# A two-block network in float32 on one core: the up units' activations turned by a VectorE block turn and ScalarE copies in place of TensorE transposes

## The chip, the cores and the metric

One core of a Trainium2 chip runs the whole kernel. The time is the device time of one launch in microseconds, the median of the runs. Five engines are named here: TensorE (PE, with its weight loads as PEld), VectorE (DVE), ScalarE (ACT), GpSimd (POOL) and SyncE (SP), which issues the weight DMAs.

## The reference, cut to what matters

Two blocks follow each other on 256 tokens of width 2048, in float32. The first is a gated mixture (linear attention and a short convolution) with a feed-forward part behind it; the second is an attention block with a layer norm. The change lies in the feed-forward part:

```python
h2 = rms_norm(x, g_ffn[l])
hid = jnp.square(jax.nn.relu(jnp.einsum('bsd,df->bsf', h2, w_ffn_up[l])))
x = x + jnp.einsum('bsf,fd->bsd', hid, w_ffn_down[l])
```

h2 is 256 x 2048, hid is 256 x 8192.

## The kernel before, in words

All large products have the same shape: 256 tokens by 2048 of contraction by 512 output columns. Such a product is a **unit**, and there are 96 of them, in the order of the list UNITS (lines 14 to 20). A unit has four **steps** of 512 of contraction, numbered s = 4u + c over the whole kernel. A step has 24 matmuls of 128x128 by 512: four tiles of contraction, two token halves, and three products, since each float32 operand is split into a high and a low part (hi x hi, hi x lo, lo x hi). The results of a unit stand in two PSUM banks, acc, one for each token half; two pairs of banks alternate.

The feed-forward part runs as four groups of four up units and four down units: up 0 to 3, down 0 to 3, up 4 to 7, down 0 to 3 again with the next 2048 of contraction, and so on.

For each step the four engines do this:

- SyncE loads 1 MB of weights, raw, three steps ahead; the load waits until VectorE has done the split of the buffer's last contents (L513).
- ScalarE makes whi, the rounded copy of raw (split, L674), two steps ahead. It waits for the load and until TensorE has left the buffer.
- VectorE makes wlo = raw - whi (split, L954).
- TensorE multiplies (products, L1390 to L1392).

Each engine goes through its own program in order. At stage s it first does split(s + 2), then what jobs(s) lists (from line 32), which is the same list for all engines. For a unit u that ends with step 4u + 3, the job "post" at that stage takes the result out of PSUM, and the table LATER (line 25) says which jobs follow at stages 4u + 4, 4u + 5 and so on. TensorE does its jobs behind the products of the same stage.

For an up unit, post is: ScalarE writes Relu of the first token half into a tmp buffer (L756) and VectorE that of the second (L1101), each scaled by the token's rstd; POOL squares the whole buffer in place (L625). The down units need the result with the features on the partitions, so the job turn_up at stage 4u + 4 turns it: TensorE makes eight 128x128 transposes into two of the four side banks (turn, L1400), ScalarE copies each bank as the high part into A_hi (hi_of, L679), VectorE subtracts to get the low part A_lo (lo_of, L961), and the bank is free again. The eight transposes stand between two steps of products in TensorE's order. The side banks are numbered in order of use by side_uses and SN.

The down units read A_hi and A_lo. The function ready gives the semaphore on which TensorE waits before it reads a part of a set for the first time: the first down unit of a group waits, at contraction tile kk, for the turn of up unit j + kk // 4, so for the group's fourth up unit at its own fourth step. The set is free for a group's up units when the last down unit of the group before is through (set_free). There are three tmp buffers, taken in turn; tmp_free gives the wait before one is written again.

Of the kernel before, what the change touches and what calls it, by code (L numbers as in the profile page):

```python
# [22 lines left out]


LATER = {"q": ("turn_qk",), "k": ("turn_qk",), "r": ("turn_r",), "cx": ("shift", "none", "conv0", "conv1"), "cb": ("turn_cb",),
         "yb": ("turn_yb",), "wo": ("turn_wo",), "up": ("turn_up",), "q2": ("none", "turn_qk2"),
         "k2": ("turn_qk2",), "y": ("none", "turn_y")}

LEVELS = (128, 64, 32, 16, 8, 4, 2, 1)
# [152 lines left out]
def two_block_program(nc, T, C, out):  # L182
# [8 lines left out]
    with ctx:  # L191
# [21 lines left out]
        whi = [at(f"whi{i}", "hi", 8 * KB * i, [128, 4, 512], f32r) for i in range(3)]  # L213
        wlo = [at(f"wlo{i}", "lo", 8 * KB * i, [128, 4, 512], f32r) for i in range(3)]

        A_hi, A_lo = (at("setA_" + n, "A", o, [128, 16, 256], f32r) for n, o in (("hi", 0), ("lo", 16 * KB)))
        B_hi, B_lo = (at("setB_" + n, "B", o, [128, 16, 256], f32r) for n, o in (("hi", 0), ("lo", 16 * KB)))

# [127 lines left out]
        s_rv, s_rq, s_ro, s_rx = sem("s_rv"), sem("s_rq"), sem("s_ro"), sem("s_rx")  # L346
        s_cw, s_shift, s_cu = sem("s_cw"), sem("s_shift"), sem("s_cu")
        s_yb, s_pq, s_xf = sem("s_yb"), sem("s_pq"), sem("s_xf")
        s_mb, s_nm, s_ex = sem("s_mb"), sem("s_nm"), sem("s_ex")
        s_pn, s_ph, s_pl = sem("s_pn"), sem("s_ph"), sem("s_pl")  # L350
        s_vh, s_yv, s_yh, s_yl = sem("s_vh"), sem("s_yv"), sem("s_yh"), sem("s_yl")
# [32 lines left out]
        def tmp_free(u):  # L384

            n = TN[u] - 3
            if n < 0:
                return s_lvl, 1
            kind, j = UNITS[TMPS[n]]
            if kind == "wo":  # L390
                return s_sq[1], 2 * j + 2
            if kind == "down":
                return s_sq[2], 2 * (j - 12) + 2
            if kind == "cc":
                return evacuated(TMPS[n] + 2)
            return full("turn", TMPS[n], 1)

        def hi_lo_of(u):
# [5 lines left out]
        def ready(u, kk):  # L404

            kind, j = UNITS[u]
            part = kk // 2
            if u == 0:
                return s_xl, kk + 1
            if kind == "ya" and j == 0:  # L410
                return seen("turn", UI["r", kk // 4], part % 2)
            if kind == "yb" and j == 0:
                return seen("turn", UI["cb", kk // 4], part % 2)
            if kind == "wo" and j == 0:
                return seen("turn", UI["yb", kk // 4], part % 2)
            if kind == "up" and j == 0:
                return seen("turn", UI["wo", kk // 4], part % 2)
            if kind == "down" and j % 4 == 0:
                return seen("turn", UI["up", j + kk // 4], part % 2)
            if kind == "q2" and j == 0:  # L420
                return seen("turn", UI["down", 12 + kk // 4], part % 2)
            if kind == "out" and j == 0:
                return s_yl, part + 1
            return None
# [43 lines left out]
        def asf(ap):  # L468
            return ap.bitcast(f32)
# [194 lines left out]
        def scalar(e):  # L664
# [37 lines left out]
            def copies(u, dst, scale):  # L702
                for b in range(2):
# [2 lines left out]
                    e.activation(dst[:, 2 * b:2 * b + 2, :], two(side[n % 4][:, :]), ACT.Copy,  # L706
                                 scale=scale).then_inc(s_read[n % 4], 1)

            def squares(u, i, j):
                tm = tmp_of(u)  # L710
                e.wait_ge(*evacuated(u))
                e.wait_ge(*tmp_free(u))
                for t in range(2):
                    e.activation(tm[:, t, :], X1[:, t, 512 * j:512 * j + 512], ACT.Square,
                                 accum_out=ssq[i][:, t, j:j + 1]).then_inc(s_sq[i], 1)
# [64 lines left out]
            for s in range(NS):  # L780
# [7 lines left out]
                for job, a in jobs(s):  # L788
# [80 lines left out]
                    elif job == "turn_cb":  # L869
                        j = UNITS[a][1]  # L870
                        e.wait_ge(*mm_done(UI["ya", 3]))
                        for b in range(2):
                            hi_of(("turn", a, b), B_hi[:, 4 * j:4 * j + 4, :], b)
                    elif job == "turn_y":
                        j = UNITS[a][1]
                        e.wait_ge(*set_free(a))
                        e.wait_ge(s_xf, 2)
                        e.wait_ge(*full("values", 11 if j < 2 else 15))
                        for b in range(2):
                            k = 4 * j + 2 * b  # L880
                            e.wait_ge(*seen("turn", a, b))
                            e.activation(A_hi[:, k:k + 2, :], YT[:, k:k + 2, :], ACT.Copy).then_inc(s_yh, 1)
                    elif job in ("turn_yb", "turn_up"):
                        j = UNITS[a][1] % 4
                        e.wait_ge(*set_free(a))
                        for b in range(2):
                            hi_of(("turn", a, b), A_hi[:, 4 * j:4 * j + 4, :], b)
                    elif job in ("turn_wo", "turn_x2"):
                        i, col = (1, G_FFN) if job == "turn_wo" else (2, G_FIN)
                        j = UNITS[a][1] % 4  # L890
                        squares(a, i, j)
                        e.wait_ge(*set_free(a))
                        for b in range(2):
                            hi_scaled(("turn", a, b), B_hi[:, 4 * j:4 * j + 4, :], col + 4 * j, b)
                        if j == 3:
                            root(i)
                    elif job == "turn_qk2":
                        kind, g = UNITS[a]
                        dst = (qTa if kind == "q2" else kTa)[g % 2]
                        if g >= 2:  # L900
                            e.wait_ge(*full("scores", 8 * (g - 2) + 7))
                        else:
                            e.wait_ge(s_xf, 2)
                        for b in range(2):
                            hi_of(("turn", a, b), dst[:, :, :], b)
                    elif job == "att":
                        if a % 2 and a >= 3 and not gate_turns(s):
                            one_half((a - 3) // 2)
                        for h in ((a - 2, a - 1) if a >= 2 and a % 2 == 0 else ()):
                            n = SN["probs", h]  # L910
                            e.wait_ge(*full("probs", h))
                            if h >= 2:
                                e.wait_ge(*full("values", h // 2 - 1))
                            e.activation(PT[h % 2][:, :, :], two(side[n % 4][:, :]), ACT.Copy).then_inc(s_ph, 1)
                        for h in ((a, a + 1) if a < 32 and a % 2 == 0 else ()):
                            b = h % 2
                            e.wait_ge(s_nm, h + 1)
                            for t in range(2):
                                e.activation(Sm[b][:, t, :], Sm[b][:, t, :], ACT.Exp, bias=nmx[b][:, t:t + 1],  # L919
                                             accum_out=den[b][:, t:t + 1]).then_inc(s_ex, 1)  # L920
                    elif job == "bank_ln":
                        e.wait_ge(s_ln, 32)
                        if a == 0:
                            for b in range(4):
                                last = max(n for n in SN.values() if n % 4 == b)
                                e.wait_ge(s_read[b], last // 4 + 1)
                        else:
                            e.wait_ge(*evacuated(UI["out", 2]))
                        for i in ((0, 1), (2,))[a]:
                            e.activation(gain_at[i], lngB[:, vcols[i]], ACT.Copy).then_inc(s_lb, 1)  # L930
                            e.activation(bias_at[i], lnbB[:, vcols[i]], ACT.Copy).then_inc(s_lb, 1)
                    elif job == "post":
                        post(a)
# [11 lines left out]
        def vector(e):  # L945
# [208 lines left out]
            def times_gate(u):  # L1154
                j = UNITS[u][1]
                e.wait_ge(*seen("values", 4 * j + 3))
                for b in range(2):
# [2 lines left out]
                    e.wait_ge(*full("turn", u, b))  # L1160
                    e.tensor_tensor(v, two(side[n % 4][:, :]), v, ALU.mult).then_inc(s_read[n % 4], 1)

            def finish(t):
                v, r, m = lvar[:, t:t + 1], lrs[:, t:t + 1], nmu[:, t:t + 1]
                e.wait_ge(s_dv, dv)
# [20 lines left out]
            for s in range(NS):  # L1186
# [17 lines left out]
                for job, a in jobs(s):  # L1204
# [101 lines left out]
                    elif job == "turn_y":  # L1306
# [3 lines left out]
                        for b in range(2):  # L1310
# [1 line left out]
                            e.wait_ge(s_yh, 2 * j + b + 1)  # L1312
                            e.tensor_tensor(A_lo[:, k:k + 2, :], YT[:, k:k + 2, :], asf(A_hi[:, k:k + 2, :]),
                                            ALU.subtract).then_inc(s_yl, 1)
                    elif job in ("turn_yb", "turn_up"):
                        j = UNITS[a][1] % 4
                        for b in range(2):
                            lo_of(("turn", a, b), A_lo[:, 4 * j:4 * j + 4, :], A_hi[:, 4 * j:4 * j + 4, :], b)
# [48 lines left out]
        def tensor(e):  # L1367
# [117 lines left out]
            for s in range(NS):  # L1485
# [6 lines left out]
                for job, a in jobs(s):  # L1492
# [37 lines left out]
                    elif job.startswith("turn"):  # L1530
# [2 lines left out]
                            e.wait_ge(s_rx, 2 * j + 2)  # L1533
                        elif kind == "yb":
                            e.wait_ge(s_yb, j + 1)
                        elif kind == "up":
                            e.wait_ge(s_pq, j + 1)
                        else:
                            e.wait_ge(*evacuated(a))
                        if kind in ("wo", "down"):  # L1540
# [77 lines left out]
```

## Time and profile before

| | |
|---|---|
| median of 3 runs | 2231.16 us (2230.51 to 2231.3) |
| span of the profiled execution | 2229.0 us |
| instructions | 24387 |
| TensorE busy | 2217.9 us, 100% |
| VectorE busy | 1274.6 us, 57% |
| ScalarE busy | 991.3 us, 44% |
| POOL busy | 225.7 us, 10% |
| DMA, mean | 200 GB/s |

The profile gives the span from the first to the last instruction of one execution; it states no other time for that execution, so the span is to be set beside the median, 2.2 us above it. A share of busy time is a mean over the whole kernel. Matmuls overlap in the trace (one lasts 0.39 us and the next starts 0.23 us after it), so their summed durations are more than the span. In the tables a row gives a source line, an engine, an operation, what it writes and reads, and how often.

### The profile page before, as it was taken

What the parts mean: (1) busy time and instruction counts of PE and PEld (TensorE: products, weight loads), DVE (VectorE), ACT (ScalarE), POOL (GpSimd) and SP (SyncE); (2) the same over time, 40 slices, a digit from 0 to 9 for tenths busy, and PEclk for the clock granted to TensorE, in tenths of its full rate; (3) what the DMA queues carried; (4) which work ended last, traced back from release to release, by engine and by line L of the source; (5) the groups of instructions that cost most, each with busy time, mean ns of one, the idle gap of its engine ahead of it and who ended that gap; (6) DMA issues with size and microseconds to landing.
All of it is one profiled execution on the core that took longest, in us unless ns stands there. A gap on an engine that the chain in (4) does not pass through costs nothing.

```text
span 2229.0 us, 24387 instructions
## 1 busy us (share of the span) xinstructions
PE 2217.9 (100%) x10314; PEld 1844.9 (83%) x10314; DVE 1274.6 (57%) x1061; ACT 991.3 (44%) x950; POOL 225.7 (10%) x253
## 2 busy tenths in 40 slices
PE   9999999999999999999999999999999999999998
PEld 8888888888888888888888888888888888888886
DVE  6577645545556545555454444554555577786755
ACT  7464654333333443344433433433444455555642
POOL 1023010000000000000000100000100121353201
PEclk9999999999999999999999999999999999999999
DMA  9554556678877766655565555555555756555663
GB/s 321 185 179 162 169 180 199 208 221 224 243 228 231 217 202 199 226 186 191 177 201 188 189 189 189 188 189 189 188 185 194 250 191 196 182 177 176 220 238 117
DMA packets 217100, 444.89 MB, mean 200 GB/s; under 512 B 9316, under 2 KB 10484, under 8 KB 216096
## 3 DMA queue, kind: packets, MB, share of 16 engines
q1 hardware_dynamic: 206976, 411.07, 56.1%
q0 software_dynamic: 9728, 32.18, 6.1%
q8 instruction: 81, 1.33, 0.2%
q14 instruction: 27, 0.22, 0.0%
q10 hardware_dynamic: 288, 0.10, 0.0%
HBM read 427.08 MB, written 12.06 MB: 197 GB/s over the span
## 4 chain that ended last, share of the span: by engine, by line
PE 100%; DVE 0%; POOL 0%; POOLq 0%; ACT 0%; issue 0%
PE acc L1390 31%; PE acc L1391 31%; PE acc L1392 31%; PE side L1400 2%; PE side L1478 1%; PE side L1414 1%; PE side L1450 1%; PE side L1464 1%; PE acc L1405 0%; PE side L1435 0%; PE side L1433 0%; PE side L1434 0%; PE side L1499 0%; PE side L1500 0%; POOL X L657 0%; PE side L1521 0%
## 5 line engine op out<-in xcount | busy, mean ns | idle before, releaser
L954 DVE TENSOR_TENSOR wlo<-raw,whi 128x2048 fp32r<-128x2048 f32 x380 | 892.1, 2348 | 739.3 <-ACT whi L674 739.2
L674 ACT ACTIVATE whi<-raw 128x2048 fp32r<-128x2048 f32 x380 | 727.7, 1915 | 784.9 <-PE acc L1392 762.2
L1390 PE MATMUL acc<-whi,setA_lo 128*128 128x512 f32 x1792 | 700.6, 391 | 0.0
L1392 PE MATMUL acc<-whi,setA_hi 128*128 128x512 f32 x1792 | 697.4, 389 | 0.0
L1391 PE MATMUL acc<-wlo,setA_hi 128*128 128x512 f32 x1792 | 697.4, 389 | 0.0
L1390 PE MATMUL acc<-whi,setB_lo 128*128 128x512 f32 x1280 | 502.9, 393 | 0.0
L1391 PE MATMUL acc<-wlo,setB_hi 128*128 128x512 f32 x1280 | 498.8, 390 | 0.0
L1392 PE MATMUL acc<-whi,setB_hi 128*128 128x512 f32 x1280 | 498.3, 389 | 0.0
L1392 PEld LDWEIGHTS acc<-whi,setA_hi 128*128 128x128 f32 x1792 | 336.4, 188 | 70.1
L1390 PEld LDWEIGHTS acc<-whi,setA_lo 128*128 128x128 f32 x1792 | 336.5, 188 | 69.9 <-DVE setA_lo L985 0.6
L1391 PEld LDWEIGHTS acc<-wlo,setA_hi 128*128 128x128 f32 x1792 | 336.6, 188 | 68.2
L1390 PEld LDWEIGHTS acc<-whi,setB_lo 128*128 128x128 f32 x1280 | 240.4, 188 | 50.6
L1392 PEld LDWEIGHTS acc<-whi,setB_hi 128*128 128x128 f32 x1280 | 240.3, 188 | 50.6
L1391 PEld LDWEIGHTS acc<-wlo,setB_hi 128*128 128x128 f32 x1280 | 240.5, 188 | 48.0
L625 POOL TENSOR_TENSOR tmp<-tmp 128x1024 f32<-128x1024 f32 x16 | 30.3, 1896 | 753.5 <-DVE tmp L1101 753.5
L568 POOL TENSOR_TENSOR bia<-bia,msk 128x512 f32<-128x512 f32 x32 | 50.1, 1567 | 80.3 <-DMA bia<-t_scratch 40.8
L919 ACT ACTIVATE Sm<-Sm,nmx 128x256 f32<-128x256 f32 x64 | 32.1, 502 | 51.7 <-DVE nmx L1361 51.7
L679 ACT ACTIVATE setA_hi<-side 128x512 fp32r<-128x512 f32 x40 | 21.8, 596 | 70.9 <-PE side L1400 70.9
L605 POOL TENSOR_TENSOR DD<-cum 128x2048 f32<-128x2048 f32 x8 | 36.4, 4553 | 146.2 <-DVE cum L1238 91.8
L1400 PE MATMUL side<-ident,tmp 128*128 128x128 f32 x352 | 45.6, 272 | 0.0
L961 DVE TENSOR_TENSOR setA_lo<-side,setA_hi 128x512 fp32r<-128x512 f32 x40 | 25.8, 686 | 34.4 <-ACT setA_hi L679 34.4
L565 POOL DMA_DIRECT2D bia<-rb_scratch x64 | 39.1, 617 | 58.6 <-DVE Sm L1354 57.1
(205 smaller groups left out, 1000.8 us busy)
## 6 DMA issues: line engine op xcount, KB each, us to landing
raw<-in_w_in SPq DMA_DIRECT2D x188, 1024.0 KB, 5.2
raw<-in_w_ffn_up SPq DMA_DIRECT2D x64, 1024.0 KB, 5.3
raw<-in_w_ffn_down SPq DMA_DIRECT2D x64, 1024.0 KB, 5.1
raw<-in_w_gla_out SPq DMA_DIRECT2D x16, 1024.0 KB, 5.2
raw<-in_w_conv_out SPq DMA_DIRECT2D x16, 1024.0 KB, 5.2
raw<-in_w_o SPq DMA_DIRECT2D x16, 1024.0 KB, 5.2
raw<-in_w_out SPq DMA_DIRECT2D x16, 1024.0 KB, 5.2
t_scratch<-t5v POOLq DMA_DIRECT2D x8, 512.0 KB, 7.3
```

Source lines behind the costliest of these rows:

```text
L565: e.dma_start(dst, src).then_inc(s_bia[b], 16)
L568: e.tensor_tensor(bia[b][:, :, :], bia[b][:, :, :], msk[h // 16][:, :, :], ALU.add).then_inc(s_mb, 1)
L605: e.tensor_tensor(dv, cv, ref, ALU.subtract).then_inc(s_xd, 1)
L625: e.tensor_tensor(tm, tm, tm, ALU.mult).then_inc(s_pq, 1)
L674: e.activation(whi[r][:, :, :], raw[r][:, :, :], ACT.Copy).then_inc(s_hi, 1)
L919: e.activation(Sm[b][:, t, :], Sm[b][:, t, :], ACT.Exp, bias=nmx[b][:, t:t + 1], accum_out=den[b][:, t:t + 1]).then_inc(s_ex, 1)
L954: e.tensor_tensor(wlo[r][:, :, :], raw[r][:, :, :], asf(whi[r][:, :, :]), ALU.subtract).then_inc(s_lo, 1)
L961: e.tensor_tensor(lo[:, 2 * b:2 * b + 2, :], two(side[n % 4][:, :]), asf(hi[:, 2 * b:2 * b + 2, :]), ALU.subtract).then_inc(s_read[n % 4], 1)
L1390: e.matmul(o, xl, whi[r][:, k, :], start=kk == 0, stop=False)
L1391: e.matmul(o, xh, wlo[r][:, k, :], start=False, stop=False)
L1392: f = e.matmul(o, xh, whi[r][:, k, :], start=False, stop=kk == 15)
L1400: f = e.transpose(bank[:, 256 * j + 128 * t:256 * j + 128 * t + 128], src(t, 2 * b + j), ident[:, :])
```

## The change

The job turn_up is replaced by two jobs, flip at stage 4u + 4 and flip_split at stage 4u + 5, in which TensorE has no part.

In flip, VectorE waits for POOL's square and turns the tmp buffer in one instruction, which transposes each 32x32 block by itself and writes to A_blk. A_blk lies where A_hi of the same four contraction tiles lies. After it the features are on the partitions within each group of 32, but a block of features 32r to 32r + 31 of a tile still stands on the partition group q of its tokens. ScalarE then moves the blocks between partition groups: 16 copies, one for each pair (q, r), each of 32 partitions by 256 elements, from A_blk to A_raw. A_raw lies where A_lo lies. Eight copies (q = 0, 1) are in flip and eight (q = 2, 3) in flip_split. Then ScalarE, once all 16 are complete, copies A_raw to A_hi (128 x 1024), and VectorE subtracts A_lo = A_raw - A_hi in place (128 x 1024).

The first down unit of a group waits for s_fs, the count of these subtractions, in place of the side banks. A tmp buffer is free again when VectorE's block turn of it is complete. In TensorE's program the wait for the square goes. The diff, without the lines that only allocate semaphores:

```diff
-         "yb": ("turn_yb",), "wo": ("turn_wo",), "up": ("turn_up",), "q2": ("none", "turn_qk2"),
+         "yb": ("turn_yb",), "wo": ("turn_wo",), "up": ("flip", "flip_split"), "q2": ("none", "turn_qk2"),
...
+        A_raw = at("setA_raw", "A", 16 * KB, [128, 16, 256])
+        A_blk = at("setA_blk", "A", 0, [128, 4, 4, 2, 4, 32])
...
+            if kind == "up":
+                return s_fl, j + 1
             return full("turn", TMPS[n], 1)
...
             if kind == "down" and j % 4 == 0:
-                return seen("turn", UI["up", j + kk // 4], part % 2)
+                return s_fs, j + kk // 4 + 1
...
+            def moves(u, quarters):
+                j = UNITS[u][1]
+                k = 4 * (j % 4)
+                for q in quarters:
+                    for r in range(4):
+                        dst = A_raw[32 * r:32 * r + 32, k:k + 4, :].rearrange("p k (t q n) -> p k t q n", t=2, q=4)
+                        e.activation(dst[:, :, :, q, :], A_blk[32 * q:32 * q + 32, j % 4, :, :, r, :],
+                                     ACT.Copy).then_inc(s_fm, 1)
...
-                    elif job in ("turn_yb", "turn_up"):
+                    elif job == "flip":
+                        e.wait_ge(s_fl, UNITS[a][1] + 1)
+                        moves(a, (0, 1))
+                    elif job == "flip_split":
+                        j = UNITS[a][1]
+                        k = 4 * (j % 4)
+                        moves(a, (2, 3))
+                        e.wait_ge(s_fm, 16 * j + 16)
+                        e.activation(A_hi[:, k:k + 4, :], A_raw[:, k:k + 4, :], ACT.Copy).then_inc(s_fh, 1)
+                    elif job == "turn_yb":
...
+            def flip(u):
+                j = UNITS[u][1]
+                e.wait_ge(*set_free(u))
+                e.wait_ge(s_pq, j + 1)
+                src = tmp_of(u)[:, :, :].rearrange("p t (k n) -> p t k n", k=4)
+                dst = A_blk[:, j % 4, :, :, :, :].rearrange("p k t r n -> p t k (r n)")
+                e.transpose(dst, src).then_inc(s_fl, 1)
...
-                    elif job in ("turn_yb", "turn_up"):
+                    elif job == "flip":
+                        flip(a)
+                    elif job == "flip_split":
+                        j = UNITS[a][1]
+                        k = 4 * (j % 4)
+                        e.wait_ge(s_fh, j + 1)
+                        e.tensor_tensor(A_lo[:, k:k + 4, :], A_raw[:, k:k + 4, :], asf(A_hi[:, k:k + 4, :]),
+                                        ALU.subtract).then_inc(s_fs, 1)
+                    elif job == "turn_yb":
...
-                        elif kind == "up":
-                            e.wait_ge(s_pq, j + 1)
```

## Rows read from the trace of the kernel before

**Rows 1.** The page, busy time by engine and the chain by engine.

```profile
PE 2217.9 (100%) x10314; PEld 1844.9 (83%) x10314; DVE 1274.6 (57%) x1061; ACT 991.3 (44%) x950; POOL 225.7 (10%) x253
...
PE 100%; DVE 0%; POOL 0%; POOLq 0%; ACT 0%; issue 0%
```

**Rows 2.** TensorE's waits: engine line <- releaser: us in total, times, longest us.

```profile
PE acc L1405 <- DVE tmp L948: 1.5, 1, 1.5
```

**Rows 3.** The chain in order of time: start us, us, what.

```profile
1083.35 0.87 PE side L1400 x8
...
1106.00 0.87 PE side L1400 x8
...
1215.70 0.87 PE side L1400 x8
```

**Rows 4.** ScalarE's timeline behind up unit 3: start us, us, instruction [idle before <-releaser].

```profile
1100.60 0.69 ACT L756 ACTIVATE tmp<-acc,rstd 128x512 f32<-128x512 f32 x1 [3.46 <-PE acc L1392]
1101.18 1.91 ACT L674 ACTIVATE whi<-raw 128x2048 fp32r<-128x2048 f32 x1
1106.54 1.09 ACT L679 ACTIVATE setA_hi<-side 128x512 fp32r<-128x512 f32 x2 [3.45 <-PE side L1400]
```

**Rows 5.** VectorE's timeline in the same stretch.

```profile
1100.60 0.75 DVE L1101 TENSOR_SCALAR tmp<-acc,rstd 128x512 f32<-128x512 f32 x1 [1.14 <-PE acc L1392]
...
1103.12 2.35 DVE L954 TENSOR_TENSOR wlo<-raw,whi 128x2048 fp32r<-128x2048 f32 x1 [1.77 <-ACT whi L674]
1107.17 1.29 DVE L961 TENSOR_TENSOR setA_lo<-side,setA_hi 128x512 fp32r<-128x512 f32 x2 [1.69 <-ACT setA_hi L679]
```

**Rows 6.** TensorE's timeline around the turn of up unit 3.

```profile
1105.61 0.39 PE L1392 MATMUL acc<-whi,setA_hi 128*128 128x512 f32 x1
1105.84 1.03 PE L1400 MATMUL side<-ident,tmp 128*128 128x128 f32 x8
1106.63 0.48 PE L1390 MATMUL acc<-whi,setA_lo 128*128 128x512 f32 x1
```

**Rows 7.** POOL's timeline in the same stretch.

```profile
1101.43 1.90 POOL L625 TENSOR_TENSOR tmp<-tmp 128x1024 f32<-128x1024 f32 x1 [20.76 <-DVE tmp L1101]
```

**Rows 8.** Groups by line and shape: count | busy us, mean ns | idle before.

```profile
L700 ACT ACTIVATE setA_hi<-XT,VT 128x256 fp32r<-128x256 f32 x16 | 8.0, 499 | 0.2
...
L840 ACT ACTIVATE Vh<-V 128x1024 fp32r<-128x1024 f32 x4 | 4.2, 1045 | 0.0
...
L803 ACT ACTIVATE wgs<-wgu 16x1024 fp32r<-16x1024 f32 x2 | 2.1, 1052 | 0.0
...
L1259 DVE TENSOR_TENSOR Vl<-V,Vh 128x1024 fp32r<-128x1024 f32 x4 | 4.9, 1216 | 0.0
...
L1015 DVE COPY SC<-side 128x512 f32<-128x512 f32 x1 | 0.7, 677 | 0.0
```

**Rows 9.** ScalarE's timeline where small copies follow each other.

```profile
87.59 0.40 ACT L800 ACTIVATE wlr<-wlr 128x256 fp32r<-128x256 f32 x1
87.89 2.13 ACT L803 ACTIVATE wgs<-wgu 16x1024 fp32r<-16x1024 f32 x2
...
1818.08 0.38 ACT L774 ACTIVATE YT<-side 64x256 f32<-64x256 f32 x1
1818.48 0.38 ACT L775 ACTIVATE YT<-side 64x256 f32<-64x256 f32 x1
1818.89 0.69 ACT L733 ACTIVATE tmp<-acc,rstd 128x512 f32<-128x512 f32 x1
```

**Rows 10.** Timelines of POOL and VectorE in the decay levels.

```profile
178.21 3.79 POOL L605 TENSOR_TENSOR DD<-cum 128x2048 f32<-128x2048 f32 x1 [5.24 <-DVE QK L1043]
...
179.46 4.69 DVE L954 TENSOR_TENSOR wlo<-raw,whi 128x2048 fp32r<-128x2048 f32 x1 [1.40 <-ACT whi L674]
```

**Rows 11.** DMA issues: count, size, median us to landing.

```profile
raw<-in_w_ffn_down SPq DMA_DIRECT2D x64, 1024.0 KB, 5.1
```

**Rows 12.** Stretch of the first group: busy by engine, PEclk, DMA share, GB/s.

```profile
1034.00:1122.00 88.00, 88.00 (x406) 73.23 (x405) 44.20 (x27) 35.51 (x27) 7.06 (x4) 1.00 0.56 188
```

More of the change, by code:

```diff
@@ L348, in two_block_program @@
         s_yb, s_pq, s_xf = sem("s_yb"), sem("s_pq"), sem("s_xf")
+        s_fl, s_fm, s_fh, s_fs = sem("s_fl"), sem("s_fm"), sem("s_fh"), sem("s_fs")
         s_mb, s_nm, s_ex = sem("s_mb"), sem("s_nm"), sem("s_ex")
```

## The prediction

> **What bounds the kernel now.** The page's busy shares come first: TensorE is at work for 2217.9 of 2229.0 us, VectorE for 57% and ScalarE for 44% [rows 1]. The chain that ended last gives TensorE 100% [rows 1], and in the list of waits TensorE waits once, for 1.5 us at the start [rows 2]. So each microsecond of TensorE that goes is a microsecond of time, as long as what feeds TensorE stays early. The other two engines have spare time in total, but the spare time lies between deadlines, so the second reading is their timelines around one up unit, against the moments at which TensorE needs what they make.
>
> The chain in order of time has one row for each turn of eight transposes [rows 3]. From the turn at 1083.35 to that at 1106.00 is one unit and one turn, 22.65 us; from 1106.00 to 1215.70 are five units and one turn, 109.70 us. The difference is four units: (109.70 - 22.65) / 4 = 21.76 us a unit, 5.44 us a step, and the turn costs 22.65 - 21.76 = 0.89 us. The row itself says 0.87; the first matmul behind a turn is a little slow.
>
> **Removed on TensorE.** 16 turns (128 transposes) by 0.89 us: 14.2 us, all on the path. With nothing late the time is 2231.2 - 14.2 = 2217.0 us. I set the sum against the profiled span, 2229.0 us; the median of the runs is 2.2 us above it, start and end of the launch, which the change leaves alone. The hi copies of ScalarE from PSUM (1.09 us a unit) and the lo subtractions of VectorE (1.29 us) go too [rows 4, 5]; both lay beside TensorE's work.
>
> **Added, and its deadline.** Let T be the start of the first step after an up unit. The turn after that step starts at 1105.84 [rows 6], so for the up unit 3, T is 1105.84 - 5.44 = 1100.40. What lies there now: Relu halves on both engines from T+0.2, ScalarE's weight split T+0.78 to T+2.69, POOL's square T+1.03 to T+2.93, VectorE's split T+2.72 to T+5.07 [rows 4, 5, 7]. With the change:
>
> - the block turn stands behind VectorE's split. No row shows one. It has 1024 elements a lane in one instruction; the bounds are 0.68 us (a copy of 512 elements from PSUM) and 2.29 us (2048 elements), and I take 1.25 us, from the subtraction with the same 1024 elements, 1.22 us [rows 8], plus a little for filling a block. It ends at T+6.25. The Trainium skill ("Vector Engine (DVE) Microarchitecture Reference", The reshape front-end and per-opcode configuration) has the transpose run at one element per cycle per lane; that would be near the value taken, and no row here shows it.
> - eight copies of ScalarE, 32 lanes by 256 elements. The nearest rows: 0.38 us for 64 lanes by 256 from PSUM, and 0.40 us for 128 lanes by 256 in SBUF [rows 9]. How they follow each other matters as much. The 128-lane copy at 87.59 is followed 0.30 us later, 0.10 us before its own end. The 64-lane copies at 1818.08, 1818.48 and the next at 1818.89 stand 0.40 and 0.41 us apart, not overlapped, and two of 16 lanes by 1024 take 2.13 us at 1.05 each [rows 8, 9]. The new copies are of the second sort, so 0.42 us each; the bounds are 0.30 and 0.50 us (a 128-lane one of 256 elements with a pointer, rows 8). Eight take 3.36 us: T+6.3 to T+9.7.
> - ScalarE's next split, due from T+5.7, waits behind them: to T+11.6, VectorE's half to T+13.9. TensorE needs it at the start of its third step, T+16.3: covered.
> - eight more copies, to T+15.0; the wait for their own completions and the hi copy of 1024 elements, 1.04 us [rows 8], to T+16.1; VectorE's lo, 1.22 us, to T+17.3.
> - the two splits behind that, delayed: ScalarE to T+18.0 and T+19.8, VectorE to T+20.2 (needed at T+21.8, covered by 1.6 us) and T+22.4 (needed at T+27.2). Their weights come 5.1 us after issue [rows 11], and each issue waits for a VectorE split three steps ahead; the latest, at T+20.2, lands at about T+25.4 and is wanted at T+27.2.
>
> Who waits for the lo at T+17.3? Of up units 0 to 2 of a group nobody. Of up unit 3 the last quarter of the contraction of the first down unit, which starts at T+16.3. The other cost is that the work is not quite done when the next up unit ends at T+21.8. VectorE's Relu half then runs from T+22.4 to T+23.1, so POOL's square lasts from T+23.2 to T+25.1, and VectorE's split cannot pass it: at 178.21 POOL held its instruction to 182.00, and VectorE's split, begun at 179.46, ended at 184.15, 2.15 us after POOL and 4.69 us long [rows 10]. So here the split ends at T+27.2, which is 5.45 of the new unit where it was 5.07. Such a loop takes about 22.2 us where a unit takes 21.76, and each up unit of a group is 0.45 us later than the one before. The fourth has its lo at 17.3 + 3 x 0.45 = 18.6; with 0.1 us to restart, TensorE stands from 16.3 to 18.6, 2.3 us, once in each of four groups: 9.2 us.
>
> **Sum.** 2231.2 - 14.2 + 9.2 = 2226.2 us, 0.22% less. This is fragile: a copy 0.02 us dearer moves each lo by 16 x 0.02 = 0.3 us plus as much again for each unit of drift, and the sum by about 5 us. The case's own range is 2221 to 2232. POOL's own work doesn't change; its issue queue has no DMA in these stages. The tmp buffer is freed by VectorE's turn where it was freed by TensorE's, at about the same time.
>
> **Rivals.**
>
> *Nothing is late.* If the copies follow each other every 0.30 us, eight take 2.4 us, two lots save 1.9 us and the loop falls below a unit, so there is no drift: lo at 17.3 - 1.9 = 15.4, before 16.3. Time 2217.0. For it: the 128-lane pair in rows 9. Against it: every row of fewer lanes. The Trainium skill ("ScalarE: Activation LUTs", What ACT_TABLE_LOAD costs) gives the overlap of ScalarE's instructions that follow each other as about 93 ns without a word on lanes. By that rule this rival is the outcome; the trace agrees for 128 lanes and not for 64 or 16.
>
> *The ScalarE and VectorE loop becomes the bound of the up units.* Place: the block turn, or the copies. If the turn takes 2.29 us (half rate), the loop is 23.2 us against 21.76, a drift of 1.5 us a unit, and the fourth lo comes at 18.3 + 4.5 = 22.8: 6.5 us late in each group, part of it paid already at the splits of units 2 and 3. That is 26 us: 2231.2 - 14.2 + 26 = 2243. It turns slower than before once a group loses more than 3.55 us, with a turn of about 1.6 us, or copies of 0.44 us. Copies of 0.50 us give by the same working some 30 us, 2247. For it: that neither form of instruction is in the trace, and that source and destination lanes differ. Against it: the 64-lane rows also cross lanes and cost no more than 0.38 us.
>
> *The change does not do what it says* would be TensorE's transposes costing nothing today. Rows 3 exclude it: a unit with a turn is longer by the turn.
>
> **Chances.** Forecast case 0.58, half of it on the faster side of its middle; nothing late 0.16; loop as the bound 0.26. A measurement of this kernel can tell about 0.2%, 4.5 us, from no change. Faster by more than that, below 2226.7: all of the second case and some 0.35 of the first, 0.51. Slower, above 2235.6: most of the third, 0.24. Within: 0.25. The range is 2216 to 2243: its low end is the floor set by the removed work, less a microsecond for what the runs differ, its high end the half-rate turn; beyond it lie dearer copies with about 0.1, and a little under the floor.
>
> **What would show it.** TensorE's 128x128 transposes on tmp drop from 352 to 224, and the distance of two up units' ends is 21.76 us. In TensorE's waits a new row appears: setA_lo, four times, about 2.3 us each, at the first down unit's fourth step. The block turn's row shows 1.2 to 1.3 us x16, the copies 0.40 us x256 with starts 0.42 us apart, and VectorE's split after an up unit of 2 to 4 in a group starts later and lasts longer than 2.35 us. If the copies stand 0.30 us apart, the second case is right; if TensorE also waits for splits (wlo) inside up units, the third. The prediction is wrong outright if TensorE waits nowhere and still doesn't gain 14 us, or if the granted clock, now 1.00 [rows 12], falls behind the new stalls.

## The result, and the profile after

The changed kernel takes 2234.38 us, the median of 19 runs (2230.16 to 2236.62), against 2230.91 us for the kernel before (2230.35 to 2231.84, 19 runs). The ratio is 1.0014, 95% interval 1.0008 to 1.0021: slower by about 3.5 us, or 0.16%, where 2226.2 us was forecast. The profiled execution took 2231.5 us with a span of 2229.7 us, so it is one of the quicker ones (the second quickest of the 19).

The removed work is gone: TensorE's instructions fall from 10314 [rows 1] to 10186, which are the 128 transposes. But the spread of the runs has grown from 1.5 us to 6.5 us, and that needs a cause of its own.

The page, busy time by engine and the chain by engine, of the changed kernel:

```profile
PE 2206.4 (99%) x10186; PEld 1831.5 (82%) x10186; DVE 1296.8 (58%) x1061; ACT 1095.0 (49%) x1190; POOL 234.5 (11%) x253
...
PE 95%; ACT 2%; DVE 1%; POOL 1%; issue 0%; DMA 0%; POOLq 0%; SPq 0%; ACTq 0%; DVEq 0%
```

ScalarE has 240 instructions and 104 us more; the chain, all TensorE before [rows 1], now runs through ScalarE, VectorE and POOL for a few per cent. TensorE's waits in the changed kernel (what waited, for whom, us in total, times, longest), and below them the groups that are new or changed:

```profile
PE acc L1429 <- DVE setA_lo L1352: 11.9, 4, 3.2
PE acc L1444 <- DVE tmp L971: 1.5, 1, 1.5
```

```profile
L720 ACT ACTIVATE setA_raw<-setA_blk 32x256 f32<-32x256 f32 x256 | 106.3, 415 | 78.0 <-DVE setA_blk L1192 72.2
L1192 DVE STREAM_TRANSPOSE setA_blk<-tmp 128x1024 f32<-128x1024 f32 x16 | 19.8, 1235 | 7.8 <-POOL tmp L630 7.8
L1352 DVE TENSOR_TENSOR setA_lo<-setA_raw,setA_hi 128x1024 fp32r<-128x1024 f32 x16 | 19.6, 1225 | 37.0 <-ACT setA_hi L905 37.0
```

The one new wait of any size against [rows 2] is the one that was foreseen: on setA_lo, four times. The block turn takes 1.24 us, the copy 0.415 us. The timelines of ScalarE and VectorE behind the fourth up unit of the first group:

```profile
1097.68 0.69 ACT L770 ACTIVATE tmp<-acc,rstd 128x512 f32<-128x512 f32 x1 [0.86 <-PE acc L1431]
1098.26 1.91 ACT L679 ACTIVATE whi<-raw 128x2048 fp32r<-128x2048 f32 x1
1105.63 3.49 ACT L720 ACTIVATE setA_raw<-setA_blk 32x256 f32<-32x256 f32 x8 [5.46 <-DVE setA_blk L1192]
1109.15 1.92 ACT L679 ACTIVATE whi<-raw 128x2048 fp32r<-128x2048 f32 x1
1111.09 3.49 ACT L720 ACTIVATE setA_raw<-setA_blk 32x256 f32<-32x256 f32 x8
1114.61 1.06 ACT L905 ACTIVATE setA_hi<-setA_raw 128x1024 fp32r<-128x1024 f32 x1
```

```profile
1037.20 1.23 DVE L1192 STREAM_TRANSPOSE setA_blk<-tmp 128x1024 f32<-128x1024 f32 x1
...
1054.76 0.74 DVE L1124 TENSOR_SCALAR tmp<-acc,rstd 128x512 f32<-128x512 f32 x1
1056.68 2.95 DVE L977 TENSOR_TENSOR wlo<-raw,whi 128x2048 fp32r<-128x2048 f32 x1 [1.18 <-ACT whi L679]
1059.55 1.23 DVE L1192 STREAM_TRANSPOSE setA_blk<-tmp 128x1024 f32<-128x1024 f32 x1
...
1078.44 3.54 DVE L977 TENSOR_TENSOR wlo<-raw,whi 128x2048 fp32r<-128x2048 f32 x1 [0.59 <-ACT whi L679]
1081.90 1.23 DVE L1192 STREAM_TRANSPOSE setA_blk<-tmp 128x1024 f32<-128x1024 f32 x1
...
1099.46 0.74 DVE L1124 TENSOR_SCALAR tmp<-acc,rstd 128x512 f32<-128x512 f32 x1
1100.20 2.29 DVE L977 TENSOR_TENSOR wlo<-raw,whi 128x2048 fp32r<-128x2048 f32 x1
1104.35 1.25 DVE L1192 STREAM_TRANSPOSE setA_blk<-tmp 128x1024 f32<-128x1024 f32 x1 [1.86 <-POOL tmp L630]
...
1115.70 1.23 DVE L1352 TENSOR_TENSOR setA_lo<-setA_raw,setA_hi 128x1024 fp32r<-128x1024 f32 x1 [2.31 <-ACT setA_hi L905]
```

Compare with [rows 4, 5]. The block turns are 22.35, 22.35 and 22.45 us apart, and a unit of TensorE takes 21.76: 0.6 to 0.7 us of delay piles up with each unit. VectorE's split in front of the turn lasts 2.95 us in the second unit and 3.54 us in the third, where [rows 5] has 2.35. This unit's T is 1097.49 (0.19 us before the first row), the lo ends at 1116.93, which is T+19.4, and it is wanted at T+16.3. POOL's square in the second and the fourth unit, and TensorE's timeline behind the pause:

```profile
1055.59 1.90 POOL L630 TENSOR_TENSOR tmp<-tmp 128x1024 f32<-128x1024 f32 x1 [20.46 <-DVE tmp L1124]
...
1100.28 3.97 POOL L630 TENSOR_TENSOR tmp<-tmp 128x1024 f32<-128x1024 f32 x1 [20.45 <-DVE tmp L1124]
```

```profile
1116.98 0.50 PE L1429 MATMUL acc<-whi,setA_lo 128*128 128x512 f32 x1 [2.90 <-DVE setA_lo L1352]
1117.32 0.48 PE L1430 MATMUL acc<-wlo,setA_hi 128*128 128x512 f32 x1
1117.60 0.63 PE L1431 MATMUL acc<-whi,setA_hi 128*128 128x512 f32 x1
1118.02 0.63 PE L1429 MATMUL acc<-whi,setA_lo 128*128 128x512 f32 x1
...
1120.16 0.63 PE L1431 MATMUL acc<-whi,setA_hi 128*128 128x512 f32 x1
1120.58 0.54 PE L1429 MATMUL acc<-whi,setA_lo 128*128 128x512 f32 x1
1120.96 0.39 PE L1430 MATMUL acc<-wlo,setA_hi 128*128 128x512 f32 x1
```

In the second unit the square ends at 1057.49 and the split begun at 1056.68 ends at 1059.63, 2.14 us later, as in [rows 10] and in the prediction (2.15).

Behind the pause of 2.9 us the matmuls start 0.43 us apart and not 0.23. The windows of this stretch say why. Each row gives the start and end in us, the length, the busy time (with the number of instructions) of PE, PEld, DVE, ACT and POOL, the granted clock of TensorE (PEclk, 1.00 is full speed), the DMA share and the GB/s:

```profile
1114.00:1116.00 2.00, 0.09 (x1) 0.00 (x0) 0.30 (x1) 1.95 (x4) 0.00 (x0) 1.00 0.53 157
1116.00:1118.00 2.00, 1.02 (x3) 0.81 (x4) 1.42 (x2) 2.00 (x2) 0.00 (x0) 0.87 0.95 368
1118.00:1120.00 2.00, 2.00 (x6) 1.58 (x5) 2.00 (x2) 1.27 (x1) 0.00 (x0) 0.50 0.00 0
1120.00:1122.00 2.00, 2.00 (x8) 1.58 (x8) 2.00 (x1) 0.00 (x0) 0.00 (x0) 0.78 0.41 78
```

The granted clock, 1.00 before the pause, is 0.50 (1.2 GHz of 2.4) from 1118 to 1120. From 1117.60 to 1120.96 there are eight distances between matmuls, 3.36 us where full clock takes 1.81: one fall costs 1.6 us. The restart itself costs 0.3 us: at the third pause, which no fall follows, the matmuls at 1470.45 and 1475.22 are seven starts and 4.77 us apart, where 1.59 is usual, so 3.18 us are lost for an idle time of 2.89. In this execution only one of the four pauses is followed by it; at the other three the granted clock stays 1.00 in all windows.

The other 18 executions have no timeline, but the record gives the mean granted clock of each, and it goes with the time. It is 0.998 in the three quickest (2230.16 to 2231.89 us), 0.997 or 0.998 in the next six (2232.93 to 2233.54) and 0.995 or 0.996 in the ten from 2234.38 up; the runs of the kernel before have 0.998 or 0.999. A fall to half for 3.4 us of 2230 lowers the mean by some 0.0008, so 0.995 to 0.996 is what three or four falls give.

So the theory to be tested had two parts. ScalarE's copies, which do not overlap, make the fourth lo late, and TensorE pauses 3 us in each group. And a pause is followed by a fall of the clock in some executions and not in others, 1.6 us a time.

### The profile page after: what moved, and what is told of

Same layout as the page of the kernel before. It is cut to its first block, busy times and chain, and to the rows that moved or that the text cites. A ratio compares the mean times of both kernels' runs of the same rounds, so it can differ in the third digit from the quotient of the medians.

```text
span 2229.7 us, 24355 instructions
## 1 busy us (share of the span) xinstructions
PE 2206.4 (99%) x10186; PEld 1831.5 (82%) x10186; DVE 1296.8 (58%) x1061; ACT 1095.0 (49%) x1190; POOL 234.5 (11%) x253
## 4 chain that ended last, share of the span: by engine, by line
PE 95%; ACT 2%; DVE 1%; POOL 1%; issue 0%; DMA 0%; POOLq 0%; SPq 0%; ACTq 0%; DVEq 0%
PE acc L1429 30%; PE acc L1430 30%; PE acc L1431 30%; PE side L1439 1%; ACT setA_raw L720 1%; DVE wlo L977 1%; POOL tmp L630 1%; ACT whi L679 1%; PE side L1517 1%; PE side L1453 1%; PE side L1489 1%; PE side L1503 1%; DVE setA_blk L1192 0%; DVE setA_lo L1352 0%; ACT setA_hi L905 0%
## 5 line engine op out<-in xcount | busy, mean ns | idle before, releaser
L720 ACT ACTIVATE setA_raw<-setA_blk 32x256 f32<-32x256 f32 x256 | 106.3, 415 | 78.0 <-DVE setA_blk L1192 72.2
L630 POOL TENSOR_TENSOR tmp<-tmp 128x1024 f32<-128x1024 f32 x16 | 38.6, 2412 | 747.6 <-DVE tmp L1124 747.6
L1352 DVE TENSOR_TENSOR setA_lo<-setA_raw,setA_hi 128x1024 fp32r<-128x1024 f32 x16 | 19.6, 1225 | 37.0 <-ACT setA_hi L905 37.0
L1120 DVE TENSOR_TENSOR X<-acc,X 128x512 f32<-128x512 f32 x40 | 25.8, 686 | 22.9 <-PE acc L1431 22.9
```

Of the source, the lines that this page charges most:

```text
L630: e.tensor_tensor(tm, tm, tm, ALU.mult).then_inc(s_pq, 1)
L720: e.activation(dst[:, :, :, q, :], A_blk[32 * q:32 * q + 32, j % 4, :, :, r, :], ACT.Copy).then_inc(s_fm, 1)
L1120: e.tensor_tensor(xv, acc[u % 2][t][:, :], xv, ALU.add).then_inc(ev, 1)
```

## The experiments

### Fewer copies, and copies on 128 lanes

```diff
-                    for r in range(4):
-                        dst = A_raw[32 * r:32 * r + 32, k:k + 4, :]...
-                        e.activation(dst[:, :, :, q, :], A_blk[32 * q:32 * q + 32, j % 4, :, :, r, :],
+                    dst = A_raw[:, k:k + 4, :]...
+                    e.activation(dst[:, :, :, q, :], A_blk[:, j % 4, :, :, q, :],
...
```

> The block turn, ScalarE's hi copy and VectorE's lo stay; the 16 copies of 32 lanes by 256 become 4 of 128 lanes by 256, which fill the same buffer but leave each block on its own partition group, so the values behind the up units are not those of the network. Theory A (the serial copies make the fourth unit's lo late, nothing else is wrong with the change): no waits of TensorE on setA_lo, granted clock 1.00 throughout, 2230.9 - 14.2 = 2216.7 us. Theory B (the block turn, the new buffers or the second stage cost something by themselves): over 2219 us with waits elsewhere.

Measured: 2216.74 us (2216.52 to 2216.93; ratio 0.9936, interval 0.9923 to 0.9950), and TensorE waits for nothing but the first memset, as in every kernel here. So 14.2 us is what the removal of the transposes is worth, and block turn, buffers and second stage add nothing to the time.

The second kernel keeps all 16 copies and makes them wider:

```diff
-                        dst = A_raw[32 * r:32 * r + 32, k:k + 4, :]...
-                        e.activation(dst[:, :, :, q, :], A_blk[32 * q:32 * q + 32, j % 4, :, :, r, :],
+                        if r == 0:
+                            dst = A_raw[:, k:k + 4, :]...
+                        else:
+                            dst = V_junk[:, 4 * (r - 1):4 * r, :]...
+                        e.activation(dst[:, :, :, q, :], A_blk[:, j % 4, :, :, r, :],
```

> All 16 copies stay, with 256 elements each and the same runs of 32, but each on 128 lanes; one in four goes to the buffer, the others to space that is unused in these stages, so the values behind the up units are not those of the network. Theory A (ScalarE overlaps copies that follow each other only on 128 lanes): starts 0.31 us apart instead of 0.44, 16 x 0.13 = 2.1 us less for a unit, no drift, lo at 17.6 - 2.1 = 15.5 us behind the unit's end, before the 16.3 where it is wanted: 2216.7 us. Theory B (the gap comes from the semaphore or from the shape): starts 0.44 us apart and about 2234 us, as with the change.

Measured: 2216.74 us (2216.12 to 2217.36; ratio 0.9936, interval 0.9921 to 0.9951), no wait on the A set. Its ScalarE timeline:

```profile
1104.19 0.42 ACT L724 ACTIVATE setA_raw<-setA_blk 128x256 f32<-128x256 f32 x1 [3.56 <-DVE setA_blk L1196]
1104.51 1.01 ACT L724 ACTIVATE V_junk<-setA_blk 128x256 f32<-128x256 f32 x3
1105.43 0.40 ACT L724 ACTIVATE setA_raw<-setA_blk 128x256 f32<-128x256 f32 x1
```

Four times the lanes, and each copy about as long as before (0.40 us against 0.415), but the next starts 0.31 us later and not 0.44. The overlap decides between 2216.7 and 2234.4 us.

Theory A's reason, the number of lanes, is not shown by this: the run also takes away every change of the starting partition and every copy between partition groups. [rows 9] speak against the number alone. At 87.89 the first of two copies on 16 lanes starts 0.10 us before the end of a 128-lane one; by the kernel's text it reads and writes partitions 0 to 15. The second writes partitions 64 to 79 and does not overlap. The 64-lane copies of [rows 9], without overlap too, go from one half of the partitions to the other. So either the change of the starting partition or the copy between groups goes with the missing overlap, and no run separates these two.

### One or two copies given to VectorE

```diff
+BY_VECTOR = ((3, 3),)              # ((3, 3), (3, 2)) for two
...
+                        if (q, r) in BY_VECTOR:
+                            continue
...
                 e.transpose(dst, src).then_inc(s_fl, 1)
+                e.wait_ge(s_fl, j + 1)
+                for q, r in BY_VECTOR:
+                    e.tensor_copy(...).then_inc(s_fm, 1)
```

(The arguments of the copy are left out.)

> The changed kernel with one of each unit's 16 copies, the last, done by VectorE behind its block turn; ScalarE does 15. Theory A (a loop of 22.35 us for a unit of 21.76 is what piles up): 15 copies make the loop 21.91 us, drift 0.15 us instead of 0.6, lo of the fourth unit at 17.57 - 0.44 + 0.45 = 17.6 us, TensorE idle 1.2 us four times, no fall of the clock: 2216.5 + 4 x 1.4 = 2222.1 us, some 12 us less for one copy in sixteen. Theory B (what counts is only the copies before the deadline, 0.44 us each): idle 2.6 us four times, above 2228 us.

> The same with two of the 16 copies done by VectorE. Theory A: loop 21.47 us, no drift, lo at 17.57 - 0.88 = 16.7 us, TensorE idle 0.3 us four times: 2216.5 + 4 x 0.5 = 2218.5 us. Theory B: idle 2.1 us four times, above 2226 us.

Measured: 2222.27 us (2222.07 to 2222.54; ratio 0.9962, interval 0.9950 to 0.9975) with one and 2218.87 us (2218.72 to 2218.88; ratio 0.9947, interval 0.9933 to 0.9961) with two. TensorE's waits with one:

```profile
PE acc L1437 <- DVE setA_lo L1360: 4.5, 4, 1.1
```

With one, the block turns of the first group start at 1037.69, 1059.60, 1081.51 and 1103.41: a loop of 21.91 us. One copy in sixteen, 0.44 us of ScalarE, is worth 12 us of the whole: four pauses of 1.1 us in place of 3.0 give some 7.5 of it, and the rest is the falls of the clock, which are gone (1.00 in all four stretches of the profiled execution). The loop is still 0.15 us longer than a unit. With two, TensorE waits 0.3 us four times, the block turns are 21.76 us apart, so nothing drifts, and the time is 3.4 us less again.

### Without the square

```diff
-                e.wait_ge(s_pq, j + 1)
+                e.wait_ge(*evacuated(u))
...
-                        e.tensor_tensor(tm, tm, tm, ALU.mult).then_inc(s_pq, 1)
```

> The changed kernel without POOL's square; the block turn waits for the two Relu halves instead, so the square of the activation is left out. Theory A (POOL's square against VectorE's split makes each unit of a group 0.6 us later than the one before, 1.9 us of the fourth's 3.1): no drift, lo 17.5 us behind the unit's end in every unit, TensorE idle 1.0 us four times, with the restart 1.3 us each: 2216.5 + 5.2 = 2221.7 us. Theory B (the copies' length alone makes the drift): still near 3 us four times, about 2231 us or more.

Measured: 2222.07 us (2221.6 to 2222.45; ratio 0.9961, interval 0.9948 to 0.9975). TensorE's wait, and VectorE behind the third unit:

```profile
PE acc L1427 <- DVE setA_lo L1350: 4.3, 4, 1.1
```

```profile
1078.17 2.29 DVE L975 TENSOR_TENSOR wlo<-raw,whi 128x2048 fp32r<-128x2048 f32 x1 [1.24 <-ACT whi L677]
1080.38 1.24 DVE L1190 STREAM_TRANSPOSE setA_blk<-tmp 128x1024 f32<-128x1024 f32 x1
```

The split lasts 2.29 us in place of 3.54, and the next block turn comes at 1102.14, 21.76 us later: no drift. So the drift needs both: the copies, which make VectorE's next Relu half and with it the square late, and the square, which then holds up VectorE's split. The row of POOL in the changed kernel shows the other order of the same: in the fourth unit VectorE begins its split first, at 1100.20, and the square begun at 1100.28 lasts 3.97 us, where [rows 7] has 1.90.

### The fourth unit of each group left to TensorE

```diff
+        if kind == "up" and j % 4 == 3:
+            later = ("turn_up",)
```

with the waits counted accordingly.

> Up units 0 to 2 of a group as with the change, unit 3 turned by TensorE as before. If only the last deadline matters: 12 x 0.89 = 10.7 us less than before, 2220.2 us. Theory A adds what the drift of three units does to the fourth: in the changed kernel the fourth square ended 6.8 us behind the unit's end, and TensorE's transposes want it at 5.44 us, so TensorE stands some 1.3 us four times: 2225.6 us, and the list of waits names tmp and POOL's square, not setA_lo.

Measured: 2226.01 us (2225.62 to 2226.34; ratio 0.9978, interval 0.9969 to 0.9986).

```profile
PE side L1448 <- POOL tmp L639: 4.4, 4, 1.1
```

Four waits of 1.1 us, with 0.3 us each for the restart, make 5.6 of the 5.8 us between 2220.2, the time by the last deadline alone, and the measured 2226.0. The deadline on the lo is gone, and the drift of three units shows at the next thing that TensorE wants of the chain, the fourth square.

### Work in place of the pause

```diff
+                if c == 3 and UNITS[u][0] == "down" and UNITS[u][1] % 4 == 0:
+                    e.wait_ge(*evacuated(u - 1))
+                    for _ in range(14):
+                        e.matmul(acc[(u - 1) % 2][0][:, 0:128], ident[:, :], ident[:, :], start=True, stop=True)
```

> The changed kernel, with 14 matmuls of 128x128 on constants, into a PSUM bank that nothing reads then, put on TensorE just before the wait for the fourth unit's lo: 14 x 0.21 = 3.0 us of work where it stood idle for 2.9 to 3.2 us. Theory A (behind an idle stretch the granted clock falls to half in some executions and not in others, 1.6 us for each time, and this makes the runs of the changed kernel differ by 6.5 us): TensorE is as late as before but the clock stays 1.00: 2216.5 + 4 x 3.3 = 2229.7 us, all runs within 1 us. Theory B (the spread comes from the weights' DMAs or from something else): runs between 2230 and 2237 us as with the change.

Measured: 2230.18 us (2229.78 to 2230.54, 11 runs; ratio 0.9997, interval 0.9988 to 1.0006). The runs differ by 0.8 us in place of 6.5. With useless work in the pause the kernel is 4.2 us faster in the median than with nothing in it. TensorE is as late as before: it starts the step 0.06 us behind the end of the lo at 1117.57 (the trace counts each of the 14 matmuls twice):

```profile
1114.57 3.29 PE L1422 MATMUL acc<-ident 128*128 128x128 f32 x28
1117.63 0.50 PE L1434 MATMUL acc<-whi,setA_lo 128*128 128x512 f32 x1
```

The window in which the changed kernel had 0.50 has here:

```profile
1118.00:1120.00 2.00, 2.00 (x10) 1.67 (x9) 1.84 (x1) 1.94 (x2) 0.00 (x0) 1.00 0.23 87
```

So neither the late lo nor the weights' DMAs, which this kernel has too, make the spread.

### A pause put into a kernel that has none

In the kernel of the next section, in which TensorE never waits for the A set, one wait is added at the same place:

```diff
+                    if k == 0 and c == 3 and UNITS[u][0] == "down" and UNITS[u][1] % 4 == 0:
+                        e.wait_ge(s_hi, split_done(s + 2))       # long pause: s_lo
```

> The kernel in which VectorE and ScalarE share the copies and TensorE waits nowhere, with one wait put on TensorE at the place where it stood in the changed kernel: for ScalarE's split of two steps ahead, which comes 2.2 to 2.4 us after that step could start. Nothing else is changed. Theory A (the idle time itself costs, and can bring the clock down): 2216.5 + 4 x 2.5 = 2226.5 us if the clock stays, up to 1.6 us more for each of four pauses if it falls.

> As the kernel with the middle pause, but the wait is for VectorE's split of two steps ahead, 4.6 us after that step could start. Theory A: 2216.5 + 4 x 4.8 = 2235.7 us for the idle time, and the clock falls behind more of the pauses than with 3 us: with all four 2242.1 us. Theory B (the clock has nothing to do with the pause): 2235.7 us and granted clock 1.00 in all stretches behind a pause.

Measured: 2229.67 us (2229.15 to 2231.6, 10 runs; ratio 0.9996, interval 0.9987 to 1.0005) and 2244.3 us (2244.02 to 2245.78; ratio 1.0063, interval 1.0048 to 1.0079).

The middle pause, 2.15 us in each group, gives 2216.5 + 4 x 2.45 = 2226.3 us without a fall (2.15 and 0.3 for the restart). No run is there. Seven stand at 2229.2 to 2229.7, which at 1.6 us a fall is two falls, with a mean granted clock of 0.997; three at 2231.1 to 2231.6, which is three, with 0.996. The profiled execution, with 2231.09 us, shows three:

```profile
1118.00:1120.00 2.00, 2.00 (x6) 1.52 (x6) 0.56 (x1) 0.00 (x0) 0.00 (x0) 0.50 0.96 334
...
1296.00:1298.00 2.00, 2.00 (x6) 1.63 (x5) 0.67 (x1) 0.00 (x0) 0.00 (x0) 0.50 0.97 331
...
1473.00:1475.00 2.00, 2.00 (x10) 1.61 (x9) 1.79 (x1) 0.00 (x0) 0.00 (x0) 1.00 0.97 348
...
1651.00:1653.00 2.00, 2.00 (x6) 1.54 (x6) 0.31 (x1) 0.00 (x0) 0.00 (x0) 0.50 0.91 291
```

All four pauses last 2.15 us; at the third, which ended at 1472.61, the clock stays. The long pause, 4.5 us, gives 2216.5 + 4 x 4.8 = 2235.7 us; the rest of the measured 2244.3 is 8.6 us, 2.1 us a pause, more than 1.6. At the first of them the clock falls while TensorE still stands (0.63 from 1116 to 1118, first matmul at 1118.75) and the matmuls are slow until about 1123. All four pauses are followed by a fall here. The theory had the direction and the place; the size was short by 2 us. The two kernels with added pauses ran on the same chip as the filled kernel, which showed no fall, so the pause and not the chip brings the falls.

### Both engines share the copies

```diff
                 e.transpose(dst, src).then_inc(s_fl, 1)
+                e.wait_ge(s_fl, j + 1)
...
+                for q in (2, 3):
+                    for r in range(4):
...
+                        e.tensor_copy(to[:, :, :, q, :], A_blk[32 * q:32 * q + 32, j % 4, :, :, r, :]).then_inc(s_fm, 1)
...
-                        moves(a, (2, 3))
                         e.wait_ge(s_fm, 16 * j + 16)
```

> VectorE does the eight copies of q = 2, 3 right behind its block turn, in the 5.5 us in which it stood idle, while ScalarE does those of q = 0, 1. Theory A: VectorE's copies take 0.41 to 0.44 us each and end at 9.8 us behind the unit's end; ScalarE's split ends at 11.7, hi at 12.8, VectorE's split at 14.0, lo at 15.2, before 16.3; the loop of a unit is 3.5 us shorter, so nothing drifts: 2216.7 us and no wait. Theory B (VectorE's copies between partition groups are slow, or they stop POOL or ScalarE): lo later than 16.3 and over 2220 us.

Measured: 2216.35 us (2216.3 to 2217.16; ratio 0.9935, interval 0.9923 to 0.9948), and no wait of TensorE on the A set. It leaves nothing of the computation out, is faster than both kernels, and stands where the removed work put the floor. VectorE's timeline behind the fourth unit, and the row of its copies:

```profile
1102.54 1.23 DVE L1191 STREAM_TRANSPOSE setA_blk<-tmp 128x1024 f32<-128x1024 f32 x1
1103.80 2.50 DVE L1197 COPY setA_raw<-setA_blk 32x256 f32<-32x256 f32 x8
1109.27 2.29 DVE L976 TENSOR_TENSOR wlo<-raw,whi 128x2048 fp32r<-128x2048 f32 x1 [2.96 <-ACT whi L679]
1111.48 1.22 DVE L1357 TENSOR_TENSOR setA_lo<-setA_raw,setA_hi 128x1024 fp32r<-128x1024 f32 x1
```

```profile
L1197 DVE COPY setA_raw<-setA_blk 32x256 f32<-32x256 f32 x128 | 36.6, 286 | 4.1
```

The copies sit in the 5.5 us in which VectorE stood idle, and the lo is done at 1112.70, T+15.2 as worked out.

## Why the prediction was wrong

2226.2 us was forecast, 0.22% less than before; 2234.38 us was measured, 0.16% more. The mechanism of the forecast case, late copies and one pause in each group, came as described; the step that failed is the clock behind the pauses, and one term was too small.

**Removed work: right.** 14.2 us; the kernels without a pause stand at 2216.4 to 2216.7, against 2217.0.

**Durations of the new operations: right.** Block turn 1.24 us (1.25 taken), hi copy 1.06 (1.04), lo 1.23 (1.22). The copy's own time is 0.415 us, and the next starts 0.44 us after its start where 0.42 was taken.

**Place of the deadline, and the drift: right in kind, short in size.** TensorE waited where it was said, four times, for setA_lo and for nothing else. The loop is 22.35 us, not 22.2, and the first lo stands at T+17.6, not 17.3: sixteen copies by 0.02 us are the 0.3 us of the first lo. About half of it reaches VectorE's next Relu half, which starts at T+22.56 (1054.76) and was put at T+22.4, and that is what the loop missed. With 3 x 0.6 of drift the fourth comes at T+19.4 instead of 18.6. TensorE is idle 2.9 to 3.2 us, and with 0.3 us for the restart each pause costs 3.3 us, where 2.3 was put. (A restart of 0.1 us was named and not added.) The prediction said itself that 0.02 us on a copy moves the sum by about 5 us; with the restart it moved it by 4 x 1.0. Its third rival even named copies of 0.44 us, the distance measured, as the border at which the change loses what it gains; 3.3 us a group stays just below the border of 3.55. In one thing the reading was wrong: VectorE's split was to come late and last longer behind units 2 to 4, but in the fourth it starts before the square and lasts 2.29 us, and the square waits instead.

**The clock: the step that failed.** "If the granted clock, now 1.00 [rows 12], falls behind the new stalls" stood at the end as something that would make the prediction wrong, and in the sum it was priced at nothing. It costs 1.6 us for each fall. The pauses alone give 2216.5 + 4 x 3.3 = 2229.7 us, the least of the 19 runs is 2230.16, and the filled kernel, with the same pauses under work, 2230.18. The median of 2234.38 lies 4.7 us above 2229.7: three falls, and its mean granted clock is 0.996, as in the profiled execution of the middle pause, which shows three. The highest, 2236.62, lies 6.9 us above, about four, with 0.995. So of the miss of 8.2 us, 4.0 us are the longer pauses, 4.7 us the clock, and 0.5 us went the other way, since the floor is 2216.5 and not 2217.0. With the pauses alone, 2229.7, the change would have been 1.2 us faster than before and inside the forecast case's own range of 2221 to 2232: the clock turned the sign. The wide range, 2216 to 2243, holds the measured time by luck, since its high end was worked out from a block turn at half rate, which did not come.

**The rivals.** Nothing late (0.16) was the outcome by the overlap of about 93 ns in the Trainium skill ("ScalarE: Activation LUTs", What ACT_TABLE_LOAD costs). The prediction found no word on lanes there; the paragraph does say that it measures tiles of 128 partitions. The run with 128 lanes agrees, with starts 0.31 us apart for copies of 0.40 us, and gives 2216.7. For the 32-lane copies between partition groups it does not hold. The loop as a bound inside the up units did not come: no wait on wlo appears. A fall of the clock had no chance of its own; it should have been a rival, with the four pauses as its place, since TensorE had not paused in these stages before and the forecast case put four pauses there.

## What to carry to other kernels

Where one engine is busy all the time, work taken off it is gained only if the helpers still meet every deadline; lay their work out against the deadlines and compare the length of their loop with the time of a unit, since a loop 0.6 us too long comes due at the end of the group with the delay of all its units. A pause of a busy TensorE can cost more than itself: here most pauses of 2 to 3 us were followed by a fall of the clock, 1.6 us each, and none of 1.1 us, so price a pause with one fall too, or fill it. When an engine is too late by a little, look for the neighbour that stands idle in that same stretch before giving the change up: here half of the copies moved from ScalarE to VectorE turned 0.16% slower into 0.65% faster.

## What the runs showed of the hardware that was not expected

- Behind a pause of 2.15 us TensorE's granted clock fell to 0.50 for three of four equal pauses in one execution, behind 2.9 to 3.2 us for one of four in another. The 1.1 us pauses (no square, one copy on VectorE) kept 1.00 in the profiled executions and gave runs within 0.9 and 0.5 us of each other, at the time that the pauses alone give. So length alone does not decide which pause is followed by a fall, and what else does was not tried.
- VectorE's copy of 32 lanes by 256 elements between partition groups takes 0.286 us and the next starts 0.31 us after its start, against 0.415 and 0.44 on ScalarE; 0.41 to 0.44 was expected. The Trainium skill ("VectorE: DVE Perf Modes", Mode 2×_2P — use both read ports for one tensor) has two results a cycle for an instruction with one source, when source and destination are in SBUF. The row agrees with twice the rate of a subtraction, by this estimate: subtractions of 2048 and 1024 elements take 2.29 and 1.22 us, so an element takes 1.04 ns and the fixed part is 0.15 us, and 256 elements at half of 1.04 ns with 0.15 us are 0.28 us.
- The block turn takes hardly longer than a subtraction of as many elements a lane: 1.24 us for 1024 against 1.22 us.
